# A third group of expert-weight slots, made of memory that is dead in the expert loop

## The reference

```
h = layer_norm(DN_ALPHA * h + mix, ln1_g[l], ln1_b[l])
scores = jax.nn.sigmoid((xf @ w_router).astype(jnp.float32))
...
_, top_idx = lax.top_k(jnp.where(expert_mask, sel_scores, -jnp.inf), TOP_K)
...
hdn = jax.nn.silu(xb @ w_gate[e]) * (xb @ w_up[e])
return hdn @ w_down[e]
...
shared = (jax.nn.silu(xf @ ws_gate) * (xf @ ws_up)) @ ws_down
return (routed + shared).reshape(b, t, d)
```

## Time and profile before

| | us |
|---|---|
| median of 3 runs | 1453.35 |
| lowest and highest | 1451.62, 1454.11 |
| the profiled execution's own time | 1451.26 |
| its span, first to last instruction | 1449.4 |

### The profile page before, as it was taken

How to read it: one execution, slowest core, us unless ns; L and a number is a source line. 1 busy time by engine, 2 the same in 40 slices (tenths; PEclk the granted TensorE clock), 3 DMA queues, 4 the chain that set the end, 5 groups by cost and what they waited for, 6 DMA issues and landing times.

```text
span 1449.4 us, 20485 instructions
## 1 busy us (share of the span) xinstructions
PE 1355.2 (93%) x7932; PEld 704.0 (49%) x7932; DVE 430.7 (30%) x1277; ACT 219.7 (15%) x546; POOL 349.0 (24%) x369
## 2 busy tenths in 40 slices
PE   8999989999999999999989999899998988898897
PEld 5755545454444444444448555445544444444443
DVE  0443452322222222222154433522222222222223
ACT  1254210010010000100021542010100100001000
POOL 2032335232222222221000313332322222222200
PEclk9999999999999999999999999999999999999999
DMA  9722439999999999999874325399999999999993
GB/s 335 300 107 88 165 99 365 409 411 410 411 411 411 411 411 411 412 412 410 317 266 172 116 88 196 113 408 408 411 408 412 412 410 409 412 412 411 411 414 127
DMA packets 108182, 475.41 MB, mean 328 GB/s; under 512 B 16260, under 2 KB 22712, under 8 KB 75232
## 3 DMA queue, kind: packets, MB, share of 16 engines
q1 hardware_dynamic: 92960, 442.73, 76.7%
q0 software_dynamic: 15168, 32.01, 6.5%
HBM read 491.21 MB, written 3.75 MB: 341 GB/s over the span
## 4 chain that ended last, share of the span: by engine, by line
PE 47%; DMA 46%; DVE 3%; issue 1%; POOL 1%; ACT 1%; POOLq 0%; SPq 0%; DVEq 0%; ACTq 0%
DMA ring<-in_w_up_dram 46%; PE bank L599 14%; PE bank L671 6%; PE bank L682 5%; PE bank L629 4%; PE bank L575 4%; PE bank L898 3%; PE bank L793 1%; PE bank L941 1%; PE bank L774 1%; PE bank L674 1%; PE bank L548 1%; PE bank L1010 1%; PE bank L783 1%; PE bank L736 0%
## 5 line engine op out<-in xcount | busy, mean ns | idle before, releaser
L599 PE MATMUL bank<-ring,region 128*64 128x256 f32 x4096 | 463.7, 381 | 61.9 <-DMA ring<-in_w_up_dram 57.2
L1829 POOL DMA_INDIRECT region<-h_rows,rank_i x256 | 255.7, 999 | 694.1 <-DVE region L1497 558.8
L599 PEld LDWEIGHTS bank<-ring,region 128*64 128x64 f32 x4096 | 299.0, 137 | 245.3 <-DMA ring<-in_w_up_dram 77.5
L575 PE MATMUL bank<-region 128*128 128x512 f32 x512 | 247.2, 606 | 1.4 <-ACT region L1111 1.4
L629 PE MATMUL bank<-ring,region 128*64 128x512 f32 x1024 | 233.9, 599 | 0.0
L1530 DVE TENSOR_TENSOR region<-region,bank 128x256 f32<-128x256 f32 x64 | 27.0, 421 | 619.5 <-ACT region L1106 619.5
L1492 DVE STREAM_TRANSPOSE region<-region 128x256 f32<-128x256 f32 x256 | 141.7, 612 | 22.4 <-DMA region<-h_rows,rank_i 18.8
L629 PEld LDWEIGHTS bank<-ring,region 128*64 128x64 f32 x1024 | 67.9, 137 | 158.1 <-issue 109.6
L1111 ACT ACTIVATE region<-bank 128x512 f32<-128x512 f32 x128 | 76.4, 597 | 436.2 <-PE bank L629 436.2
L575 PEld LDWEIGHTS bank<-region 128*128 128x128 f32 x512 | 87.3, 190 | 89.1 <-issue 85.9
L1106 ACT ACTIVATE region<-bank 128x256 f32<-128x256 f32 x64 | 24.5, 383 | 486.5 <-PE bank L599 486.5
(11 more groups left out here) (208 smaller groups left out, 827.4 us busy)
## 6 DMA issues: line engine op xcount, KB each, us to landing
ring<-in_w_gate_dram SPq DMA_DIRECT2D x64, 2048.0 KB, 28.1
ring<-in_w_up_dram SPq DMA_DIRECT2D x64, 2048.0 KB, 28.6
ring<-in_w_down_dram SPq DMA_DIRECT2D x64, 2048.0 KB, 26.8
ring<-in_w_in_dram SPq DMA_DIRECT2D x8, 2048.0 KB, 21.0
ring<-in_w_o_dram SPq DMA_DIRECT2D x4, 2048.0 KB, 12.5
ring<-in_w_in_dram SPq DMA_DIRECT2D x4, 1024.0 KB, 15.8
region<-h_rows,rank_i POOLq DMA_INDIRECT x256, 6.1
ln_par<-in_ln_g_dram POOLq DMA_DIRECT2D x4, 512.0 KB, 6.1
```

The lines of the kernel that those rows point to most:

```text
L575: last = mm(bank[SUM_BANKS[n][half]][0:w, :], selg[:, u, t0:t0 + w], y_sb[:, u, half * 512:(half + 1) * 512], start=False, stop=stop, skip ...
L599: last = mm(bank[5][64 * e:64 * e + 64, part * F:(part + 1) * F], xgT[:, u, kk, 64 * e:64 * e + 64], w[:, e, kk, :], start=(kk == 0), stop ...
L1829: pool.indirect_dma_start(out=xg[:, u, b, :], out_offset=None, in_=h_rows, in_offset=bass.IndirectOffsetOnAxis(ap=rank_i[:, at:at + 1], ax ...
```

## The change

A third group of three slots is added, and pairs take the groups in turn: pair p uses group p mod 3. The new slots have no memory of their own. `h_tok`, `hT`, `region` and the four small weights become parts of one allocation, `arena`, and each new slot lies on two halves of 2048 floats that are not used while the experts run:

- slot 6 (gate): the tail of `region` from 10240 on, and the four small weights
- slot 7 (up): the place where `y` was, and the router's scratch
- slot 8 (down): `h_tok` and the first 1024 floats of `hT`

`y` moves onto the shared expert's down weights, and `sg`, `ha`, `h`, `h2` onto a later part of `hT`. A part of pair p is now loaded when the same part of pair p - 3 has been used. SP loads pair 2 ahead of the loop, each part behind a wait for the last readers of its memory. The small loads of layer 1 move to where the last gate product out of slot 6 is done. TensorE's loop body holds six pairs, and pairs 26 to 31 are written out behind it. VectorE's and ScalarE's loops stay as they are.

```diff
-            def load_pair(l, r, i, u, part, first):
-
-                s = part + 3 * u
-                if not first:
-
+            def load_part(l, p, group, part, freed=None):
+
+                s = 3 * group + part
+                if freed is not None:
                     used, per = ((gates_used[l], 1), (gu_done[l], 1), (y_done[l], 2))[part]
-                    sp.wait_ge(used, per * (r * PAIRS + i * 2 + u - 1))
+                    sp.wait_ge(used, per * freed)
...
-                load_pair(l, 0, 0, 0, 2, True)
+                load_part(l, 0, 0, 2)
+                sp.wait_ge(router_sums, l * 2 + 2)
+                sp.wait_ge(gate_ready, RET_ALL[l])
+                sp.wait_ge(h_ready_tok, NORM[(l, 0)][2])
+                load_part(l, 2, 2, 0)
                 sp.wait_ge(gates_ready, l + 1)
...
+                sp.wait_ge(shared_done, SHARED[l][0 if l == 0 else 2])
+                sp.wait_ge(chosen_turned, l + 1)
+                sp.wait_ge(gates_stored, (48, 80)[l])
+                load_part(l, 2, 2, 1)
+                sp.wait_ge(sums_open, l + 1)
+                sp.wait_ge(h_stored, (48, 80)[l])
+                sp.wait_ge(gathered[0][l], 64)
+                load_part(l, 2, 2, 2)
                 hold_here(sp, count_ready, l + 1)
                 most = sp.value_load(count_i[0:1, 0:1], min_val=0, max_val=T)
-                with sp.Fori(1, PAIRS // 2) as i:
-                    for u in range(2):
+
+                def load_pairs(r):
+                    with sp.Fori(1, PAIRS // 3) as i:
+                        for group in range(3):
+                            for part in range(3):
+                                load_part(l, i * 3 + group, group, part, r * PAIRS + i * 3 + group - 2)
+                    for p in range(PAIRS - 2, PAIRS):
                         for part in range(3):
-                            load_pair(l, 0, i, u, part, False)
+                            load_part(l, p, p % 3, part, r * PAIRS + p - 2)
...
+                def six_pairs(i):
+
+                    for at in range(2, 8):
+                        pair(i * 6 + at, at % 2, at % 3, i * 2 + at // 3)
+
+                pair(0, 0, 0, 0, opens=True)
+                pair(1, 1, 1, 0)
+                with pe.Fori(0, PAIRS // 6 - 1) as i:
+                    six_pairs(i)
+                six_pairs(PAIRS // 6 - 1)
...
-                round_(l, 0, load_next if l + 1 < DEPTH else None)
+                round_(l, 0)
...
+                if l + 1 < DEPTH:
+                    pool.wait_ge(gates_used[l], PAIRS - 2)
+                    load_mix(l + 1)
+                    load_moe(l + 1)
```

More of the change, by code:

```diff
@@ L288, in decoder_kernel @@
         w_o_in = [sem(f"w_o_in{n}") for n in range(2)]
-        slot_in = [sem(f"slot_in{s}") for s in range(6)]
+        slot_in = [sem(f"slot_in{s}") for s in range(9)]
         small_mix = sem("small_mix")
@@ L634, in round_, with pair @@
-                two_pairs(0, first=True)
-                with pe.Fori(1, PAIRS // 2 - 1) as i:
-                    two_pairs(i)
-                two_pairs(PAIRS // 2 - 1, final=True)
+                def pair(p, u, group, turn, opens=False):
+                    base = 3 * group
+                    arrived = ((l * ROUNDS + r) * LOADS[group] + turn) * 16 + 16
+                    pe.wait_ge(slot_in[base], arrived)
+                    pe.wait_ge(xt_ready[l], r * 32 + p + 1)
+                    if not opens:
+                        pe.wait_ge(h_ready[l], r * 32 + p)
+                    for part in range(2):
+                        if part == 1:
+                            pe.wait_ge(slot_in[base + 1], arrived)
+                        w = slot(base + part).rearrange("p e (k f) -> p e k f", k=KC)
+                        for kk in range(KC):
+                            for e in range(2):
+                                last = mm(bank[5][64 * e:64 * e + 64, part * F:(part + 1) * F],
+                                          xgT[:, u, kk, 64 * e:64 * e + 64], w[:, e, kk, :],
+                                          start=(kk == 0), stop=(kk == KC - 1))
+                        last.then_inc((gates_used[l], gu_done[l])[part], 1)
+                    if not opens:
+                        pe.wait_ge(y_ready[l], r * 64 + p * 2)
+                        pe.wait_ge(selg_ready[l], r * 32 + p)
+                        scatter(l, 1 - u, 1, 0)
+                        scatter(l, 1 - u, 1, 1)
+                        scatter(l, 1 - u, 2, 0)
+                        if l == 0:
+                            scatter(l, 1 - u, 0, 0)
+                    elif shared_piece:
+                        for at in range(3):
+                            shared_piece(at)
+                    pe.wait_ge(h_ready[l], r * 32 + p + 1)
+                    for j in range(2):
+                        last = pe.transpose(bank[7][:, j * 128:(j + 1) * 128], mo["h"][:, j * 128:(j + 1) * 128], ident)
+                    last.then_inc(ht_done[l], 1)
+                    if not opens:
+                        scatter(l, 1 - u, 2, 1).then_inc(scattered[l], 1)
+                    elif shared_piece:
+                        shared_piece(3).then_inc(scattered[l], 1)
+                    pe.wait_ge(ht_ready[l], r * 32 + p + 1)
+                    pe.wait_ge(slot_in[base + 2], arrived)
+                    w = slot(base + 2).rearrange("p e (j n) -> p e j n", j=2)
+                    for half in range(2):
+                        for j in range(2):
+                            for e in range(2):
+                                last = mm(bank[6 + half][64 * e:64 * e + 64, :],
+                                          mo["h2"][:, j * 128 + 64 * e:j * 128 + 64 * e + 64],
+                                          w[:, e, j, half * 512:(half + 1) * 512], start=(j == 0), stop=(j == 1))
+                        last.then_inc(y_done[l], 1)
```

148 lines of the change are left out of this document (59 added, 89 removed).

## The result

| | us |
|---|---|
| before, median of 4 runs beside it | 1453.73 (1451.62 to 1454.52) |
| after, median of 4 runs | 1406.64 (1403.75 to 1408.69) |
| ratio, 95% interval | 0.9677, 0.9653 to 0.9701 |
| the profiled execution after, its span | 1404.73, 1402.9 |

The kernel is 47.1 us faster. The forecast was a gain of 29.6 us and a range down to 1419.5, so the direction is right and 17 us of gain were not foreseen.

What follows compares the result with a forecast made beforehand. Both expert loops were taken as bound by DMA, ending when the last weights land. Extra pair -30.6 us, small loads +1.0, other terms 0: -29.6 from 1453.35, so 1423.8 us; 8-in-10 range 1419.5 to 1432.

Steps and rivals of the forecast that it cites:

- The extra pair ahead, -15.3 us per layer: Expert loops: one pair fewer to load after the stream starts, 6.29 MB at 411 GB/s; -30.6 us for both layers.
- At 411 GB/s: Expert loops: the DMA rate used to price one pair's 6.29 MB at 15.3 us.
- GB/s should stay at 411: Expert loops: a sign to look for in the profile after, an unchanged DMA rate.
- Small loads, +1.0: Layer 1's six small loads, moved behind pair 29's gate products: net +1.0 us, bounds 0 and +4.9.
- Pair 2's loads, 0: Ahead of and early in each loop: PE loses 0 to 3 us per layer, covered by slack; 0.
- later first products: Start of a loop: the prediction is wrong if a loop's first products come later.
- PE's six-pair body, 0: PE's expert loop: refetching the larger body could cost 6 to 18 us per layer, a loss of 0 to 5.7; taken as 0.
- Rivals 1 and 2: PE's loops. First: code streamed, PE stalls, 1490 us, 4%. Second: jumps or gathers in the way, 1436 us, 9%.
- Rival 3: Start of the stream: something holds it, so the third group adds no pair; 1453 us, chance 2%.
- The slack: Loop ends: DMA excess over PE's need left after the gain, 12.6 us in layer 0 and 28.8 in layer 1.
- Where the chain enters DMA: Expert loops: the chain of waits turns to DMA at about pair 18 in layer 0, pair 14 in layer 1.
- The upper end of the forecast's own range: Whole kernel: 1429.5 us, from 14.96 us per pair, +4.9 us of small loads and 2 us of jumps.

Runs made afterwards that it cites:

- e17: The kernel after with the arena moved by 128 B, off the 512-byte grid like the ring: 1424.19 us, ratio 0.9804 to the kernel before.
- e2: The kernel after with nine slots in turn but no extra pair ahead, pair 2 loaded when pair 1 is under way: 1449.79 us, ratio 0.9864.
- e19: The kernel after once more, unchanged: 1404.97 us, ratio 0.9686 to the kernel before.
- e16: The kernel after with ring and arena both moved onto the 512-byte grid: 1402.20 us, ratio 0.9568 to the kernel before.
- e4: As e1, but layer 1's small loads stay where the change puts them: 1457.32 us, ratio 0.9934 to the kernel before.
- e1: The kernel after without its third group of slots and with the small loads back at their earlier place: 1457.85 us, ratio 0.9928.
- e6: The kernel after run again, unchanged: 1405.74 us, ratio 0.9668 to the kernel before.
- e5: The kernel before run again, unchanged, for its profile: 1451.80 us, one run.
- e12: The kernel before with two small tiles (384 B) declared ahead of the ring, which then starts on a multiple of 512: 1441.39 us, ratio 0.9830.
- e9: The kernel before with other tiles declared between its six ring slots, nothing else changed: 1441.72 us, ratio 0.9814.
- e11: The kernel after with its six ring slots spaced by other tiles as in e9: 1416.97 us, ratio 0.9643 to the kernel before.
- e7: The kernel before with the ring declared last, 114 KB further up in each partition: 1454.51 us, ratio 1.0013.
- e18: The kernel before with 448 B of small tiles declared behind region, putting only the gathers' targets on the grid: 1440.69 us, ratio 0.9921.
- e13: The kernel before with one 128 B tile declared ahead of the ring, which then starts at 256 modulo 512: 1441.59 us, ratio 0.9832.
- e10: The kernel before with its slots used in physical order 0, 2, 4, 1, 3, 5: 1468.88 us, ratio 0.9999.
- e14: e9 with slots 1 to 5 pushed off the grid by 128 B: 1468.09 us, ratio 1.0010 to the kernel before.

## Why the prediction was right in direction and too small

1. **The extra pair ahead, -15.3 us per layer: right.** Measured alone it is 28.8 us (e17 against before on one chip, 1453.02 - 1424.19), and 27.2 in the loops of e2 against the kernel after. In the loops of e17 it is 479.67 - 465.22 = 14.5 us in layer 0 and 477.85 - 461.78 = 16.1 in layer 1, 30.5 together.
2. **The step that failed is a factor in the same term.** "At 411 GB/s" was taken for the whole stream after the change, and "GB/s should stay at 411" was written as what would show it. The rate was read from slots that start at 128 modulo 256. The change puts a third of the loads (all but slot 7's second half) and all gathers on addresses that are multiples of 256: 418 GB/s, worth 19.0 us in the loops (927.0 in e17, 908.0 after), or 20.9 against e19 on e17's chip. I had looked at what the new slots lie on, and not at where they start. No row of before could show it, since all targets in its loops were off the grid; but the bounds of the term came from 411 alone, and a term that multiplies 950 us of stream should have had the rate's own bounds.
3. **The Trainium skill has a rule that bears on it, and I did not weigh it.** "DMA: Bandwidth & Descriptors", section "How a descriptor splits into AXI transactions", says that a transaction has to start at a multiple of 256 bytes, so that a descriptor which doesn't has its first transaction start at the boundary below, and the bytes fetched there for nothing still cost; it speaks of what a transaction reads. My estimate from that rule: 8192 B from 128 would take 33 instead of 32 transactions (+3.1%), 4096 B 17 instead of 16 (+6%), and a gather's 1280 B 6 instead of 5 (+20%). Measured over 300 to 600 us, with all targets off the grid (e17) and all on it (e16): 8 KB packets 319.1 and 309.1 ns (+3.2%), 4 KB packets 164.9 and 159.1 (+3.6%), the gathers' packets of 5120 B 208.1 and 196.1 (+6%), and the rate 410 and 424 GB/s, 3.4%. Rule and runs agree in the place (256, not 128) and for the 8 KB packets in size. For the 4 KB packets the runs show a little over half of the estimate and for the gathers less than a third, and there the measurement decides.
4. **Small loads, +1.0: not to be seen** (e4 beside e1; layer 0's loop 472.57 and 472.72 us). That speaks for the lower bound, 0, but the medians can't tell 0 from 1.0.
5. **Pair 2's loads, 0: right.** The first product of pair 1 came at 233.61 (after), 232.60 (e6), 233.46 (e19), against 231.39 and 232.51 (e5) before: 0 to 2.2 us later, and none of it reached the end but through the start of the stream. The bound of 3 us holds. The prediction named later first products as a sign of being wrong; they came later, and the term held all the same (e17: pair 1 at 233.28), so that sign was too strict.
6. **PE's six-pair body, 0: right.** The pace is 15.05 and 14.34 us per pair as before, and the stretch from 1000 to 1300 us above shows one q8 packet; from 300 to 600 us there are two, where before had none in either. q8 rose from 28 to 39 packets in all, most of them outside the steady loop. Rivals 1 and 2 needed stalls in the loop; there are none. Rival 3 falls with the measured gain.
7. **The slack.** I left 12.6 us in layer 0. The pair ahead used 15 of its 27.9, the rate another 10, and 455.24 - 30 x 15.05 = 3.7 us are left. A further gain for DMA helps layer 1 alone, as e16 shows.
8. **Where the chain enters DMA.** Forecast 18 and 14. With the rate of before (e17) it is 21 and 16, with the change 28 and 18. The sign was right; the count was coarse even where the term was right.
9. **A slip in the sum.** The upper end of the forecast's own range, by its own terms, is 1453.35 - 29.92 + 4.9 + 2 = 1430.3, not 1429.5. It bears on nothing here.

## What to carry to other kernels

When a change moves the target of a DMA, compare the start addresses modulo 256 before and after, and give the rate a term of its own in the sum; a stream of 950 us turns 2% of rate into 19 us. In a kernel bound by loads, a few hundred bytes of small tiles declared ahead of the big buffers can be worth nearly as much as a rewrite: e12 gains 26 us over before with two lines moved, the extra pair ahead 28.8. And an experiment that succeeds as expected can do so for another reason: e9 confirmed a wrong theory, and only the run expected to repeat it (e11) told.

## What the runs showed of the hardware that was not expected

**The grid.** Loads from HBM into slots at 0 or 256 modulo 512 run at 423 to 424 GB/s, at 128 (or 64 above a multiple of 128, e7) at 410 to 411. The prices of single targets don't add up, though. With the ring off the grid, putting the gathers' targets on it (5% of the bytes) is worth 4 GB/s (e18 against before). With the ring on it, it is worth at most 1: in e12 and e13 the gathers' targets are still at 448, and the rate is 423 against e16's 424. And in e18 the weights' own packets became quicker although the ring had not moved: 316.4 and 163.2 ns (8 KB and 4 KB, mean over 300 to 600 us) against 319.5 and 164.1 before. So a load off the grid costs more where what is written beside it is off the grid too.

Left open: in the kernel after, slot 0 is quick (311 ns) though it starts at 128, and slot 7's second half starts at 192 modulo 512 and shows no loss. It looks as if a packet's time depends on what was written before it and not only on its own address; no run tried that apart. That the cause is the number of transactions, and not another effect with the same grid, is the Trainium skill's account and was not measured.

**The head of the loops.** On the chips where the kernel before took 1467 us, the first pair of each loop is slower. The stretch 215 to 240 us of e10 there (columns: PE, PEld, DVE, ACT, POOL busy, granted clock, DMA share, GB/s):

```profile
215.00:240.00 25.00, 20.17 (x104) 8.83 (x106) 6.85 (x20) 0.98 (x2) 13.04 (x17) 0.86 0.61 189
```

and of e5, the kernel before on the other chip:

```profile
215.00:240.00 25.00, 23.80 (x180) 13.22 (x173) 7.97 (x23) 1.96 (x4) 17.98 (x20) 1.00 0.83 298
```

A mean of 0.86 means that part of the stretch ran at 1.2 GHz and the rest at 2.4. But the lower clock is not shown to be the cause. In e10 the clock was 1.00 from 215 to 226 us and 0.51 only from 226 to 233, and pair 0's products already stood apart before it fell, with idle gaps of 0.3 to 1.5 us for which the profile names nothing. In e14, on the chip of e12, the clock was 1.00 over the whole stretch, and pair 1 was nearly as late:

```profile
215.00:240.00 25.00, 20.72 (x133) 10.10 (x134) 8.64 (x23) 1.77 (x4) 17.73 (x20) 1.00 0.62 214
```

Its pair 0 took 19.4 us from its first product to pair 1's (219.19 to 238.59), e5's 15.9 (216.49 to 232.34). What causes the gaps stays open. Their effect is plain: pair 1 starts at 240.82 in e10 instead of 232.51, the stream of weights with it, and the same again in layer 1 (963.45 instead of 947.27). That is the 16.3 us between the two profiled executions, and it is why ratios across kernels on those chips carry a few us that don't come from the edit.
